# Depthwise convolution moved from ScalarE and GpSimd to TensorE, one tap at a time between other matmuls

## The chip, the core and the metric

The kernel runs on one core of a Trainium2 chip. The metric is the device time of one execution in microseconds (us); the number given is the median of several. The engines of the core are named as in the profile: PE is TensorE (PEld its weight loads), DVE is VectorE, ACT is ScalarE, POOL is GpSimd, and SP is the engine whose queue issues the DMAs. PE writes its results to PSUM, which has eight banks of 512 float32 per partition; everything else lies in SBUF.

## The reference

Two layers of an encoder trunk work on 512 prompt positions and on 8 streams of 16 positions each, 640 columns in all. Each layer is a half-step feed-forward block, a token mixer and a second half-step feed-forward block. The mixer has three groups: sparse attention with an indexer that selects the top 128 or 132 keys of each query, a gated linear recurrence, and a convolution module. The change touches the last:

```python
def conformer_conv(glu, buf, conv_w, conv_b, ln_g, ln_b):
    a, gate = jnp.split(glu, 2, axis=-1)
    u = a * jax.nn.sigmoid(gate)
    u_pad = jnp.concatenate([buf.astype(u.dtype), u], axis=1)
    y = lax.conv_general_dilated(u_pad, conv_w[:, None, :], window_strides=(1,), padding='VALID',
                                 feature_group_count=C_CONV) + conv_b      # 31 taps, 256 channels
    y = jax.nn.silu(layer_norm(y, ln_g, ln_b))
```

Beside it the indexer's scores are `sum over heads of w * relu(qi . ki)`, of which the largest are selected; the recurrence is a sum over pairs of positions within a chunk, each with the product of the decays between them.

## The kernel before

Channels lie on the partitions and the 640 positions along the free axis, so the 256 channels of the convolution are two groups `g` of 128 partitions. All arithmetic is float32. Each layer runs as a row of blocks with a barrier between them; the block in question is `select_and_recur` (line 728), once per layer. Each engine has its own instruction list in it and waits on semaphores.

PE (line 870) first transposes some tiles (line 873), then computes 24 logit products, `for n, (t, hd) in enumerate(units)` (line 884): one matmul of 256, 384 or 512 columns each (line 892), in a ring of three banks. ACT takes each through a relu (line 1033), and DVE adds it, weighted, to the scores (lines 1099 and 1102). Then come the eight streams (line 899): logits of stream b (lines 908 and 909, four half-size matmuls), a relu on ACT (line 1051), and a weighting matmul of 512 and one of 16 columns, one iteration later (lines 917 and 919); the last of them completes the count `mixed`.

The recurrence is computed by levels m = 0, 1, 2, 4, 8, 16, 32. `prods` lists 33 level products, five in each of the levels up to 8 and four in each of the last two; each is two matmuls of 256 columns (line 938) into bank `n % 8`. DVE waits until a level's products are all there (line 1173), then folds the decays into the operands `qz` and `kp` for the next level (line 1178 for m = 0, lines 1199, 1203 and 1205 otherwise), which PE needs before it starts that level's products, then copies the level's products out of PSUM (lines 1160 and 1164), and then does one or two selection steps.

A selection step finds and removes the eight largest scores in each live row block: `max` (line 1129) and `match_replace` (line 1139). There are 28 steps for the streams and the prompt together: 12 ahead of the levels, of which the last takes the streams' scores (line 1124, after `mixed`), the rest beside the levels and behind them. DVE then makes the masks (line 1223) and the states of the recurrence (lines 1231 to 1255), PE the outputs of the recurrence (lines 980 to 1002).

The convolution runs beside this. POOL first makes the gated input `up` and `us` (lines 842 and 844). ACT scales it by one tap, for the prompt and the streams (`scale_tap`, lines 1017 and 1018), into a ring of three buffers `product`, and POOL adds the product to `yc` (line 860): 62 scalings and 60 additions per layer. ACT issues two scalings beside each stream's relu and the rest behind.

Of the kernel before, what the change touches and what calls it, by code (L numbers as in the profile page):

```python
# [63 lines left out]
def build(nc, ins, outs):  # L64
    stack = ExitStack()
    with stack:
# [661 lines left out]
        def select_and_recur(l):  # L728
# [2 lines left out]
            rb = carve(3, LALL)  # L731
            wall = carve(NS, 128)
            icb = carve(2, PAST)
            product = carve(3, TOK)
            top8 = carve(4, 8)
            s0 = carve(NS, 2, 128)
            kiz = arena[:, ARENA - 1024:ARENA - 1024 + SEQ]
            qis = proj[:, NPROJ, 0:512].rearrange("p (b n) -> p b n", b=NS)
            (tok_mm, vnew_mm, wall_mm, tok_ready, vnew_ready, wall_ready, kid_ready, logits, relu_done, weighed,
             mixed, barred, topped, replaced, masks, ic_in, gate_sig, glu_ready, conv_in, padded, conv_out, tap_scaled,  # L740
             tap_added) = (
                sem(f"sel_{n}") for n in (
                    "tok_mm", "vnew_mm", "wall_mm", "tok_ready", "vnew_ready", "wall_ready", "kid_ready", "logits",
                    "relu_done", "weighed", "mixed", "barred", "topped", "replaced", "masks", "ic_in", "gate_sig",
                    "glu_ready", "conv_in", "padded", "conv_out", "tap_scaled", "tap_added"))
            ic_in1, qis_ready, tabs_in = sem("sel_ic_in1"), sem("sel_qis_ready"), sem("sel_tabs_in")
            ic_sems = [ic_in, ic_in1]
            units = [(t, hd) for t in range(1, NEW) for hd in range(8)]
# [24 lines left out]
            o = mix[:, 4:6]  # L773
            um = flat(proj[:, 0:4])[:, 0:2048].rearrange("p (b g n) -> p b g n", b=NS, g=2)
            snew = im.rearrange("p g b n -> p (g b n)").rearrange("p (b g n) -> p b g n", b=NS, g=2)
            osq = product[:, 0:2]
            (s0_in, q_act, sig_f, sig_k, gate_act, lb_ready, f_ready, k_ready, level_mm, scored, folded_q, folded_k,
             folded_t, im_ready, kst_mm, kst_ready, u_mm, u_ready, state, new_ready, o_mm, o_copied,
             o_squared, osum_mm, oroot, saved) = (sem(f"rec_{n}") for n in (
# [17 lines left out]
            with nc.Block() as block:  # L797
# [35 lines left out]
                @block.gpsimd  # L833
                def _(pool):
                    pool.memset(kid[0:64], 0.0).then_inc(padded, 1)
                    pool.wait_ge(padded, 1)
                    pool.memset(kiz[64:128], 0.0).then_inc(padded, 1)
                    pool.wait_ge(padded, 2)
                    pool.memset(up[:, :, 0:TAPS - 1], 0.0).then_inc(padded, 1)
                    for g in range(2):  # L840
                        pool.wait_ge(gate_sig, g + 1)
                        pool.tensor_tensor(up[:, g, TAPS - 1:], proj[:, CA + g, 0:SEQ], proj[:, CG + g, 0:SEQ],
                                           ALU.mult).then_inc(glu_ready, 1)
                        pool.tensor_tensor(us[:, g, :, TAPS - 1:],
                                           proj[:, CA + g, SEQ:].rearrange("p (b i) -> p b i", b=NS),
                                           proj[:, CG + g, SEQ:].rearrange("p (b i) -> p b i", b=NS),
                                           ALU.mult).then_inc(glu_ready, 1)
                    pool.wait_ge(logits, NIDX)
                    pool.wait_ge(qis_ready, 1)
                    for rows_, a in own:  # L850
                        pool.memset(qz[rows_, :, 1 - a], 0.0).then_inc(padded, 1)
                        pool.wait_ge(padded, 4 + a)

                    for g in range(2):
                        for w in range(1, TAPS):
                            n = g * (TAPS - 1) + w - 1
                            pool.wait_ge(tap_scaled, g * TAPS + w + 1)
                            if w >= 2:
                                pool.wait_ge(tap_added, n)
                            pool.tensor_tensor(yc[:, g], yc[:, g], product[:, n % 3], ALU.add).then_inc(tap_added, 1)  # L860
                    pool.wait_ge(mixed, NS)

                    for g in range(2):
                        pool.tensor_tensor(im[:, g],
                                           tok[:, 4:5, 128 + 128 * g:256 + 128 * g].to_broadcast([128, NS, 128]),
                                           batchmask.unsqueeze(2).to_broadcast([128, NS, 128]),
                                           ALU.mult).then_inc(im_ready, 1)

                @block.tensor
                def _(pe):  # L870
# [4 lines left out]
                    for b in range(NS):  # L875
# [1 line left out]
                                          proj[:, VA, SEQ + LS * b:SEQ + LS * b + LS], ident)  # L877
                    mm.then_inc(vnew_mm, 1)
                    pe.matmul(ps[:, 7, 0:128], headsel[64:72, :], proj[64:72, KI, SEQ:], start=True,
                              stop=True).then_inc(wall_mm, 1)  # L880

                    pe.wait_ge(kid_ready, 2)
                    pe.wait_ge(padded, 3)
                    for n, (t, hd) in enumerate(units):
                        keys, _ = keys_of(t)
                        if n < 3:
                            pe.wait_ge(tok_ready, n + 1)
                        else:
                            pe.wait_ge(relu_done, n - 2)

                        ki = kid if hd % 2 else kiz
                        pe.matmul(ps[:, n % 3, 0:keys], proj[:, QI + hd // 2, 128 * t:128 * t + 128], ki[:, 0:keys],
                                  start=True, stop=True).then_inc(logits, 1)

                    pe.wait_ge(tok_ready, 5)
                    pe.wait_ge(vnew_ready, 2)
# [2 lines left out]
                    for b in range(NS + 1):  # L899
# [13 lines left out]
                        if b > 0:  # L913
# [4 lines left out]
                                      stop=(c == NS - 1))  # L918
                            pe.matmul(ps[:, 5, 0:LS], wall[:, c], rb[:, (NIDX + c) % 3, PAST:], start=(c == 0),
                                      stop=(c == NS - 1)).then_inc(mixed, 1)  # L920

                    for n, (m, t) in enumerate(prods):
                        if n == 4:
# [7 lines left out]
                        else:  # L931
                            i = levels.index(m) - 1
                            pe.wait_ge(folded_q, fold_count(i))
                            pe.wait_ge(folded_k, fold_count(i) - 1)
                        if n >= 8:
                            pe.wait_ge(scored, n - 7)
                        for g in range(2):
                            mm = pe.matmul(ps[:, n % 8, 256 * g:256 * g + 256], kp[:, g, 128 * t:128 * t + 128],  # L938
                                           qz[:, g, :, 128 * t:128 * t + 128], start=True, stop=True)
                        mm.then_inc(level_mm, 1)  # L940

                    pe.wait_ge(scored, NP)
                    pe.wait_ge(folded_k, fold_count(6) - 1)
# [61 lines left out]

                @block.scalar
                def _(act):
                    def scale_tap(m):

                        g, w = divmod(m, TAPS)  # L1010
                        n = g * (TAPS - 1) + w - 1
                        tap, *srcs = tap_of(g, w)
                        if w and n >= 3:
                            act.wait_ge(tap_added, n - 2)
                        outs_ = conv_parts(product[:, n % 3] if w else yc[:, g])
                        bias = par[:, P_CB + g:P_CB + g + 1] if w == 0 else 0.0
                        act.activation(outs_[0], srcs[0], ACT.Identity, scale=tap, bias=bias)  # L1017
                        act.activation(outs_[1], srcs[1], ACT.Identity, scale=tap, bias=bias).then_inc(tap_scaled, 1)  # L1018
# [9 lines left out]
                    for n, (t, hd) in enumerate(units):  # L1028
                        keys, _ = keys_of(t)
                        act.wait_ge(logits, n + 1)  # L1030
                        if n >= 3:
                            act.wait_ge(weighed, n - 2)
                        act.activation(rb[:, n % 3, 0:keys], ps[:, n % 3, 0:keys], ACT.Relu).then_inc(relu_done, 1)

                    act.wait_ge(tok_mm, 5)
                    act.activation(flat(f), flat(kp), ACT.Sigmoid).then_inc(sig_f, 1)
# [6 lines left out]
                    for b in range(NS):  # L1043
# [8 lines left out]
                        if b == 0:  # L1052
                            act.wait_ge(glu_ready, 4)
                            act.wait_ge(padded, 3)
                            act.wait_ge(conv_in, 32)
                        scale_tap(2 * b)
                        scale_tap(2 * b + 1)
                    for m in range(2 * NS, 2 * TAPS):
                        scale_tap(m)
                    for t in range(5):  # L1060
                        act.wait_ge(kst_mm, t + 1)
                        act.activation(kst[:, t], ps[:, t, 0:256].rearrange("p (g n) -> p g n", g=2),
                                       ACT.Copy).then_inc(kst_ready, 1)
                    act.wait_ge(tap_added, 2 * (TAPS - 1))
                    for n, t in enumerate((4, 0, 1, 2, 3)):
                        act.wait_ge(o_mm, n + 1)
                        src = ps[:, n % 4, 0:256].rearrange("p (g n) -> p g n", g=2)
# [7 lines left out]
                def _(dve):  # L1075
# [8 lines left out]
                    dve.wait_ge(wall_mm, 1)  # L1084
# [69 lines left out]
                    def keep_scores(i, m, at, k):  # L1154

                        t = prods[at + k][1]
                        dst = sc[:, t].rearrange("p (a g i) -> p g a i", a=2, g=2)
                        src = ps[:, (at + k) % 8].rearrange("p (g a i) -> p g a i", g=2, a=2)
# [559 lines left out]
```

## Time and profile before

| | before |
|---|---|
| median of 3 runs | 3256.18 us (3256.08 to 3257.55) |
| span of the profiled execution, first to last instruction | 3254.3 us |
| PE busy | 2851.5 us, 88% of the span |
| DVE busy | 1528.1 us, 47% |
| ACT busy | 944.0 us, 29% |
| POOL busy | 476.2 us, 15% |
| the block of layer 1 | 744.0 to 944 us of the span |
| the block of layer 2 | 2332 to 2532 us of the span |

The profile gives no time of the profiled execution other than its span; what lies around the span is taken as the difference to the median, 1.9 us. Busy shares are averages over the whole execution: nearly all of PE's time lies in the feed-forward blocks, which the change does not touch. The 200 us blocks have to be read by themselves.

### The profile page before, as it was taken

The numbers are of one execution on the slowest core, as the hardware profiler recorded it, in microseconds if no ns is written. First come the engines' busy times: TensorE is split into PE (matmuls) and PEld (weight loads), VectorE is DVE, ScalarE is ACT, GpSimd is POOL, SyncE is SP. The second block draws the span as 40 slices with busy tenths as digits, with TensorE's granted clock in tenths as the row PEclk, the third lists the DMA queues.
The fourth block names the chain that finished last, engine by engine and source line by source line (L and its number), as shares of the span: only waits on it lengthen the run. The fifth ranks groups of instructions, "written<-read, shape, count | busy, mean of one in ns | idle before, by whom it ended". The sixth has DMA issues, their size and how long they took to land. (4 is left out here: it accounts for less than half of the span.)

```text
span 3254.3 us, 44093 instructions
## 1 busy us (share of the span) xinstructions
PE 2851.5 (88%) x18054; PEld 2665.5 (82%) x18054; DVE 1528.1 (47%) x1886; ACT 944.0 (29%) x1237; POOL 476.2 (15%) x328
## 2 busy tenths in 40 slices
PE   1999998997477979999969999989955788999997
PEld 1899998894354879999969999979834458999997
DVE  1633333528965353333353333352499644433333
ACT  1322223216423332212232212231362342322221
POOL 1100001105812120000120000020084313000001
PEclk9999999998768989999989999999976798999998
DMA  5122212113010212122112122122120111212211
GB/s 108 65 71 71 78 63 79 65 52 98 1 73 7 72 52 78 59 83 73 57 60 84 62 81 77 57 73 78 36 76 15 59 46 46 78 68 75 78 61 63
DMA packets 50676, 209.51 MB, mean 64 GB/s; under 512 B 13928, under 2 KB 14312, under 8 KB 34568
## 3 DMA queue, kind: packets, MB, share of 16 engines
q1 hardware_dynamic: 50568, 208.05, 19.3%
q8 instruction: 70, 1.15, 0.1%
q14 instruction: 38, 0.31, 0.0%
HBM read 197.85 MB, written 10.19 MB: 64 GB/s over the span
## 5 line engine op out<-in xcount | busy, mean ns | idle before, releaser
L291 PE MATMUL ps<-hr,wr 128*128 128x320 f32 x11424 | 1707.5, 311 | 83.6 <-DVE hr L407 65.7
L291 PEld LDWEIGHTS ps<-hr,wr 128*128 128x128 f32 x11424 | 1692.3, 189 | 99.7 <-DVE hr L407 43.5
L291 PE MATMUL ps<-hid,wr 128*128 128x320 f32 x4224 | 620.8, 309 | 0.0
L291 PEld LDWEIGHTS ps<-hid,wr 128*128 128x128 f32 x4224 | 619.8, 188 | 0.0
L286 DVE TENSOR_TENSOR wr<-stage,wr 128x2048 fp32r<-128x2048 f32 x184 | 421.7, 2292 | 299.7 <-ACT wr L282 299.7
L282 ACT ACTIVATE wr<-stage 128x2048 fp32r<-128x2048 f32 x184 | 350.6, 1905 | 557.5 <-PE ps L291 288.9
L548 DVE TENSOR_TENSOR arena<-ps,arena 128x640 f32<-128x640 f32 x88 | 72.5, 824 | 545.5 <-PE ps L291 543.8
L523 POOL TENSOR_TENSOR arena<-arena 128x640 f32<-128x640 f32 x28 | 44.3, 1582 | 1737.0 <-ACT arena L499 1737.0
L490 ACT ACTIVATE arena<-arena 128x640 f32<-128x640 f32 x88 | 65.1, 739 | 801.8 <-DVE arena L548 801.8
L860 POOL TENSOR_TENSOR proj<-proj,arena 128x640 f32<-128x640 f32 x120 | 200.1, 1669 | 33.6 <-ACT arena L1018 16.9
L938 PE MATMUL ps<-proj 128*128 128x256 f32 x264 | 90.9, 519 | 97.5 <-issue 78.4
L938 PEld LDWEIGHTS ps<-proj 128*128 128x128 f32 x264 | 70.2, 273 | 117.5 <-issue 82.1
L556 DVE TENSOR_TENSOR hid<-arena,hid 128x640 f32 x88 | 72.6, 825 | 91.8 <-ACT hid L492 91.8
L1017 ACT ACTIVATE arena<-arena,par 128x512 f32<-128x512 f32 x120 | 86.5, 721 | 79.6 <-POOL proj L860 79.6
L380 POOL TENSOR_TENSOR arena<-arena 128x640 f32<-128x640 f32 x48 | 95.6, 1992 | 85.9 <-ACT arena L367 82.4
L563 DVE COPY arena<-ps 128x640 f32 x32 | 26.4, 825 | 164.0 <-PE ps L291 164.0
L621 DVE TENSOR_TENSOR proj<-ps,arena 128x640 f32 x20 | 16.5, 825 | 171.6 <-PE ps L291 171.0
L1428 ACT ACTIVATE arena<-arena 128x128 f32<-128x128 f32 (+4 forms) x80 | 47.7, 596 | 154.4 <-DVE arena L1486 154.4
L492 ACT ACTIVATE hid<-arena 128x640 f32 x88 | 65.1, 740 | 92.7 <-DVE arena L554 92.7
L336 PE MATMUL ps<-ones,arena 128*128 128x1 f32 x70 | 17.6, 320 | 84.7 <-DMA par<-in_params 66.4
L336 PEld LDWEIGHTS ps<-ones,arena 128*128 128x128 f32 x70 | 16.2, 286 | 87.3 <-DMA par<-in_params 67.9
L499 ACT ACTIVATE arena<-arena 128x640 f32 (+1 forms) x32 | 23.6, 739 | 196.3 <-DVE arena L565 196.3
(204 smaller groups left out, 2224.5 us busy)
## 6 DMA issues: line engine op xcount, KB each, us to landing
stage<-in_wgu SPq DMA_DIRECT2D x88, 1024.0 KB, 4.8
stage<-in_wd SPq DMA_DIRECT2D x32, 768.0 KB, 4.2
stage<-in_w_in SPq DMA_DIRECT2D x24, 1024.0 KB, 4.8
stage<-in_wd SPq DMA_DIRECT2D x32, 640.0 KB, 3.8
stage<-in_w_out SPq DMA_DIRECT2D x8, 1024.0 KB, 5.0
arena<-in_ic SPq DMA_DIRECT2D x16, 256.0 KB, 2.8
hf<-bias_table SPq DMA_DIRECT2D x2, 2048.0 KB, 10.7
arena<-in_kc SPq DMA_DIRECT2D x16, 256.0 KB, 5.2
```

What stands on the lines that cost most here:

```text
L282: act.activation(wr[:, j, 0], stage[:, j], ACT.Copy).then_inc(w_hi, 1)
L286: dve.tensor_tensor(wr[:, j, 1], stage[:, j], wr[:, j, 0].bitcast(F32), ALU.subtract).then_inc(w_lo, 1)
L291: mm = pe.matmul(out, w(s), v(t), start=start and n == 0, stop=stop and n == 2)
L380: pool.tensor_tensor(ssum, ssum, sqb[:, k % 2], ALU.add).then_inc(self.summed, 1)
L490: act.activation(sg[:, 0], sg[:, 0], ACT.Silu).then_inc(silu, 1)
L492: act.activation(hid_view(i, j, 0), sg[:, 1], ACT.Copy).then_inc(hid_hi, 1)
L548: dve.tensor_tensor(halves(sg[:, 0]), ps[:, 4 * j:4 * j + 2, 0:HALF], rs2, ALU.mult).then_inc(g_scaled, 1)
L556: dve.tensor_tensor(hid_view(i, j, 1), sg[:, 1], hid_view(i, j, 0).bitcast(F32), ALU.subtract).then_inc(hid_ready, 1)
L860: pool.tensor_tensor(yc[:, g], yc[:, g], product[:, n % 3], ALU.add).then_inc(tap_added, 1)
L938: mm = pe.matmul(ps[:, n % 8, 256 * g:256 * g + 256], kp[:, g, 128 * t:128 * t + 128], qz[:, g, :, 128 * t:128 * t + 128], start=True, sto ...
L1017: act.activation(outs_[0], srcs[0], ACT.Identity, scale=tap, bias=bias)
L1428: act.activation(pb[:, u % 3, 0:keys], pb[:, u % 3, 0:keys], ACT.Exp, scale=-1.0, bias=low[:, u:u + 1], accum_out=norm[:, u:u + 1]).then_i ...
```

## The change

For each group and tap ACT makes a 128x128 matrix with the tap's 128 weights on the diagonal (`diagonal`, in a ring of five buffers). PE multiplies the gated input, shifted by the tap, with it, once for the prompt (512 columns, bank 6) and once for the streams (128 columns, bank 7), and accumulates the 31 taps of a group in PSUM (`conv_tap`). One such tap is put behind each logit product from the fifth on (taps 0 to 19), behind each of the nine iterations over the streams (20 to 28) and behind each level product (29 to 61). ACT copies a finished group out of PSUM with the bias added (`conv_to_sbuf`); the first tap of the second group waits for that. The level products use a ring of six banks in place of eight. The scalings on ACT and the additions on POOL are gone.

```diff
@@ gpsimd
-                    for g in range(2):
-                        for w in range(1, TAPS):
...
-                            pool.tensor_tensor(yc[:, g], yc[:, g], product[:, n % 3], ALU.add).then_inc(tap_added, 1)
@@ tensor
+                    def conv_tap(m):
+                        g, w = divmod(m, TAPS)
+                        _, prompt, sample = tap_of(g, w)
+                        if m == 0:
+                            pe.wait_ge(vnew_ready, 2)
+                            pe.wait_ge(wall_ready, 1)
+                            pe.wait_ge(glu_ready, 4)
+                            pe.wait_ge(padded, 3)
+                            pe.wait_ge(conv_in, 32)
+                        if w == 0 and g:
+                            pe.wait_ge(conv_done, g)
+                        pe.wait_ge(diag_ready, m + 1)
+                        pe.matmul(ps[:, 6, :], diag[:, m % NDIAG], prompt, start=(w == 0), stop=(w == TAPS - 1))
+                        pe.matmul(ps[:, 7, 0:NS * LS], diag[:, m % NDIAG], sample, start=(w == 0),
+                                  stop=(w == TAPS - 1)).then_inc(tap_mm, 1)
@@ the logit products
+                        if n >= 4:
+                            conv_tap(n - 4)
@@ the streams
+                        conv_tap(NIDX + b - 4)
@@ the level products
-                        if n >= 8:
-                            pe.wait_ge(scored, n - 7)
+                        if n >= NBANK:
+                            pe.wait_ge(scored, n - NBANK + 1)
...
                         mm.then_inc(level_mm, 1)
+                        conv_tap(NIDX + NS + 1 + n - 4)
@@ scalar
-                    def scale_tap(m):
...
+                    def diagonal(m):
+                        g, w = divmod(m, TAPS)
+                        tap, *_ = tap_of(g, w)
+                        if m >= NDIAG:
+                            act.wait_ge(tap_mm, m - NDIAG + 1)
+                        act.activation(diag[:, m % NDIAG], ident, ACT.Identity, scale=tap).then_inc(diag_ready, 1)
+                    def conv_to_sbuf(g):
+                        act.wait_ge(tap_mm, TAPS * (g + 1))
+                        act.wait_ge(glu_ready, 4)
+                        bias = par[:, P_CB + g:P_CB + g + 1]
+                        act.activation(yc[:, g, 0:SEQ], ps[:, 6, :], ACT.Identity, bias=bias)
+                        act.activation(yc[:, g, SEQ:], ps[:, 7, 0:NS * LS], ACT.Identity, bias=bias).then_inc(conv_done, 1)
...
                         act.activation(rb[:, n % 3, 0:keys], ps[:, n % 3, 0:keys], ACT.Relu).then_inc(relu_done, 1)
+                        if n >= 1:
+                            diagonal(n - 1)
...
-                        scale_tap(2 * b)
-                        scale_tap(2 * b + 1)
-                    for m in range(2 * NS, 2 * TAPS):
-                        scale_tap(m)
+                        diagonal(n - 1)
+                    for m in range(NIDX + NS - 1, 2 * TAPS):
+                        diagonal(m)
+                        if m == TAPS + 1:
+                            conv_to_sbuf(0)
+                    conv_to_sbuf(1)
...
-                    act.wait_ge(tap_added, 2 * (TAPS - 1))
```

## Rows read from the trace of the kernel before

**Rows 1.** Windows of layer 1's block: length, busy us of each engine, PEclk, DMA.

```profile
core 0: us, PE busy (x) PEld busy (x) DVE busy (x) ACT busy (x) POOL busy (x), PEclk, DMA share, GB/s
744.00:766.00 22.00, 20.01 (x80) 11.91 (x82) 19.14 (x38) 16.23 (x31) 5.48 (x8) 1.00 0.23 60
766.00:796.50 30.50, 21.73 (x96) 10.82 (x97) 29.86 (x92) 26.40 (x45) 20.25 (x15) 0.83 0.48 157
796.50:898.50 102.00, 45.70 (x133) 35.25 (x133) 100.83 (x158) 47.63 (x94) 85.36 (x50) 0.72 0.09 19
898.50:944.00 45.50, 35.00 (x162) 25.75 (x162) 28.58 (x55) 7.53 (x17) 0.00 (x0) 0.62 0.07 26
```

**Rows 2.** Timeline of DVE, levels of layer 1: start, us, line, operation [idle before].

```profile
802.81 0.69 DVE L1124 COPY arena<-ps 128x528 f32<-128x528 f32 x1
...
807.80 4.27 DVE L1178 TENSOR_TENSOR proj<-proj 64x1280 f32<-64x1280 f32 x2
...
819.35 3.62 DVE L1199 TENSOR_TENSOR proj<-proj 64x640 f32<-64x640 f32 x2
...
834.38 3.49 DVE L1199 TENSOR_TENSOR proj<-proj,arena 64x640 f32<-64x640 f32 x2
...
841.61 3.21 DVE L1164 COPY_PREDICATED hf<-lvl,ps 128x512 f32<-128x512 int32 x5
...
848.94 3.67 DVE L1199 TENSOR_TENSOR proj<-proj,arena 64x640 f32<-64x640 f32 x2
...
875.96 2.10 DVE L1199 TENSOR_TENSOR proj<-proj,stage 64x256 f32<-64x256 f32 x2 [0.60 <-PE ps L938]
...
891.97 0.84 DVE L1199 TENSOR_TENSOR proj<-proj,stage 64x256 f32<-64x256 f32 x2
892.84 0.42 DVE L1203 TENSOR_TENSOR proj<-proj,stage 128x256 f32<-128x256 f32 x1
...
894.55 1.49 DVE L1209 TENSOR_TENSOR proj<-proj 128x1280 f32<-128x1280 f32 x1
...
913.46 2.48 DVE L1231 TENSOR_TENSOR proj<-ps,cst 128x512 f32<-128x512 f32 x4
```

**Rows 3.** Timeline of POOL in layer 1's block.

```profile
750.93 0.51 POOL L844 TENSOR_TENSOR arena<-proj 128x128 f32<-128x128 f32 x1
...
776.05 108.52 POOL L860 TENSOR_TENSOR proj<-proj,arena 128x640 f32<-128x640 f32 x60 [8.47 <-ACT arena L1018]
```

**Rows 4.** Timeline of PE and ACT, logit products of layer 1.

```profile
751.67 13.47 PE L892 MATMUL ps<-arena,proj 128*128 128x256 f32 x36 [1.17 <-ACT arena L1033]
...
764.32 0.60 ACT L1033 ACTIVATE arena<-ps 128x512 f32<-128x512 f32 x1 [0.26 <-PE ps L892]
765.17 0.60 ACT L1033 ACTIVATE arena<-ps 128x512 f32<-128x512 f32 x1 [0.26 <-PE ps L892]
```

**Rows 5.** Timeline of PE, sums of one column each at the full clock.

```profile
558.17 0.35 PE L336 MATMUL ps<-ones,arena 128*128 128x1 f32 x2 [1.94 <-PEq L437]
558.38 0.36 PE L337 MATMUL ps<-ones,arena 128*128 128x1 f32 x2
```

**Rows 6.** The page's costliest groups: form, count, busy us, mean ns, idle before.

```profile
L1018 ACT ACTIVATE arena<-arena,par 128x128 f32<-128x128 f32 x120 | 46.9, 391 | 0.0
```

**Rows 7.** Timeline of ACT and PE, streams of layer 1.

```profile
773.30 0.59 ACT L1051 ACTIVATE arena<-ps 128x528 f32<-128x528 f32 x1
...
773.95 2.07 PE L917 MATMUL ps<-arena 128*128 128x512 f32 x2 [5.90 <-ACT arena L1051]
...
781.12 1.12 PE L917 MATMUL ps<-arena 128*128 128x512 f32 x2
...
783.39 1.12 PE L917 MATMUL ps<-arena 128*128 128x512 f32 x2
```

**Rows 8.** Timeline of PE, level products of layer 1.

```profile
803.56 1.13 PE L938 MATMUL ps<-proj 128*128 128x256 f32 x4 [1.62 <-DVE arena L1124]
...
840.05 6.68 PE L938 MATMUL ps<-proj 128*128 128x256 f32 x20 [7.60 <-issue]
```

**Rows 9.** A window within the logit products of layer 1, columns as in Rows 1.

```profile
750.00:753.00 3.00, 1.83 (x8) 0.85 (x7) 2.58 (x5) 1.15 (x4) 1.45 (x2) 1.00 0.03 11
```

More of the change, by code:

```diff
@@ L733, in select_and_recur @@
             icb = carve(2, PAST)
-            product = carve(3, TOK)
+            osq = carve(2, TOK)
+            NDIAG, NBANK = 5, 6
+            diag = carve(NDIAG, 128)
             top8 = carve(4, 8)
@@ L738, in select_and_recur @@
             qis = proj[:, NPROJ, 0:512].rearrange("p (b n) -> p b n", b=NS)
-            (tok_mm, vnew_mm, wall_mm, tok_ready, vnew_ready, wall_ready, kid_ready, logits, relu_done, weighed,
-             mixed, barred, topped, replaced, masks, ic_in, gate_sig, glu_ready, conv_in, padded, conv_out, tap_scaled,
-             tap_added) = (
+            (tok_mm, vnew_mm, tok_ready, vnew_ready, wall_ready, kid_ready, logits, relu_done, weighed,
+             mixed, barred, topped, replaced, masks, ic_in, gate_sig, glu_ready, conv_in, padded, conv_out, diag_ready,
+             tap_mm, conv_done) = (
                 sem(f"sel_{n}") for n in (
-                    "tok_mm", "vnew_mm", "wall_mm", "tok_ready", "vnew_ready", "wall_ready", "kid_ready", "logits",
+                    "tok_mm", "vnew_mm", "tok_ready", "vnew_ready", "wall_ready", "kid_ready", "logits",
                     "relu_done", "weighed", "mixed", "barred", "topped", "replaced", "masks", "ic_in", "gate_sig",
-                    "glu_ready", "conv_in", "padded", "conv_out", "tap_scaled", "tap_added"))
+                    "glu_ready", "conv_in", "padded", "conv_out", "diag_ready", "tap_mm", "conv_done"))
             ic_in1, qis_ready, tabs_in = sem("sel_ic_in1"), sem("sel_qis_ready"), sem("sel_tabs_in")
@@ L775, in select_and_recur @@
             snew = im.rearrange("p g b n -> p (g b n)").rearrange("p (b g n) -> p b g n", b=NS, g=2)
-            osq = product[:, 0:2]
             (s0_in, q_act, sig_f, sig_k, gate_act, lb_ready, f_ready, k_ready, level_mm, scored, folded_q, folded_k,
@@ L852, in _ @@
                         pool.wait_ge(padded, 4 + a)
-                    for g in range(2):
-                        for w in range(1, TAPS):
[L856 to L859, printed above, removed]
-                            pool.tensor_tensor(yc[:, g], yc[:, g], product[:, n % 3], ALU.add).then_inc(tap_added, 1)
                     pool.wait_ge(mixed, NS)
@@ L879, in _ @@
                     pe.matmul(ps[:, 7, 0:128], headsel[64:72, :], proj[64:72, KI, SEQ:], start=True,
-                              stop=True).then_inc(wall_mm, 1)
+                              stop=True).then_inc(vnew_mm, 1)
+                    def conv_tap(m):
[13 more added lines that the diff above has]
+                                  stop=(w == TAPS - 1)).then_inc(tap_mm, 1)
                     pe.wait_ge(kid_ready, 2)
@@ L934, in _ @@
                             pe.wait_ge(folded_k, fold_count(i) - 1)
-                        if n >= 8:
-                            pe.wait_ge(scored, n - 7)
+                        if n >= NBANK:
+                            pe.wait_ge(scored, n - NBANK + 1)
                         for g in range(2):
-                            mm = pe.matmul(ps[:, n % 8, 256 * g:256 * g + 256], kp[:, g, 128 * t:128 * t + 128],
+                            mm = pe.matmul(ps[:, n % NBANK, 256 * g:256 * g + 256], kp[:, g, 128 * t:128 * t + 128],
                                            qz[:, g, :, 128 * t:128 * t + 128], start=True, stop=True)
                         mm.then_inc(level_mm, 1)
+                        conv_tap(NIDX + NS + 1 + n - 4)
                     pe.wait_ge(scored, NP)
@@ L1007, in _ @@
                 def _(act):
-                    def scale_tap(m):
+                    def diagonal(m):
                         g, w = divmod(m, TAPS)
[L1011 to L1018, printed above, removed]
+                        tap, *_ = tap_of(g, w)
[8 more added lines that the diff above has]
+                        act.activation(yc[:, g, SEQ:], ps[:, 7, 0:NS * LS], ACT.Identity, bias=bias).then_inc(conv_done, 1)
                     act.activation(kid[64:128, :], proj[0:64, KI], ACT.Copy).then_inc(kid_ready, 1)
@@ L1051, in _ @@
                         act.activation(rb[:, n % 3], flat(ps[:, q:q + 2])[:, 0:LALL], ACT.Relu).then_inc(relu_done, 1)
[L1052 to L1055, printed above, removed]
-                        scale_tap(2 * b)
-                        scale_tap(2 * b + 1)
-                    for m in range(2 * NS, 2 * TAPS):
-                        scale_tap(m)
+                        diagonal(n - 1)
[4 more added lines that the diff above has]
+                    conv_to_sbuf(1)
                     for t in range(5):
@@ L1083, in _ @@
                                         ps[0:LS, 5 + a, :].rearrange("p (b n) -> p b n", b=4)).then_inc(vnew_ready, 1)
-                    dve.wait_ge(wall_mm, 1)
+                    dve.wait_ge(vnew_mm, 2)
                     dve.wait_ge(tabs_in, 16)
@@ L1157, in keep_scores @@
                         dst = sc[:, t].rearrange("p (a g i) -> p g a i", a=2, g=2)
-                        src = ps[:, (at + k) % 8].rearrange("p (g a i) -> p g a i", g=2, a=2)
+                        src = ps[:, (at + k) % NBANK].rearrange("p (g a i) -> p g a i", g=2, a=2)
                         if m == 0:
```

## The prediction

> **What bounds the kernel now.** I read the page's busy shares first and then left them: 88% of PE's time lies mostly in the feed-forward blocks, which the change leaves alone. Both blocks that it touches take 200 us, and layer 2 repeats layer 1 within 0.1 us at every mark I compared, so I work on layer 1 and double. The windows by stage [rows 1] show which engine ends last in each: in the logit products PE is busy 20.0 of 22 us; from there to the end of the levels DVE is busy 29.9 of 30.5 and 100.8 of 102 us; in the tail PE again. So a change is worth something if it shortens DVE's list between 766 and 898 us, or PE's before and after it. ACT and POOL end nowhere last: taking work from them buys nothing by itself.
>
> Next I read DVE's timeline in the levels for operations whose price varies. The pair at line 1199 on 64x256 takes 2.10 us at 875.96 and 0.84 us at 891.97, the same shape [rows 2]. What differs is POOL: its additions run from 776.05 for 108.5 us, to 884.6 [rows 3]. The same holds for line 1203. Copies out of PSUM and selection steps don't show it. So POOL's additions, which nobody waits for, lengthen DVE's folds, whose two inputs both lie in SBUF. That is where the change can gain.
>
> **The price of a tap on PE.** A 512-column float32 matmul costs 0.86 us at the full clock: the relus of two successive logit products, which wait for PE, are 0.85 to 0.86 us apart [rows 4]. The 128-column part is two passes like any float32 matmul; by columns that is a quarter, 0.21 us, and the pairs that only load weights and stream one column are 0.21 to 0.22 us apart [rows 5], so 0.22 either way. A tap is 1.08 us. Bounds: 0.86 if the 128 columns hide entirely; 1.29 if a load shows at two of the four passes (0.11 each, half of that pair). I take 1.08, since in the logit products loads are hidden.
>
> The Trainium skill ("TensorE: Matmul & The Clock Gate", Part 3, "The mechanism") says that weight loads overlap matmuls in flight only when they address other rows of the array. Diagonals fill all rows. By that rule every load would show, and a tap would cost far more; here the rule does not agree with rows 4, where full-height logit products follow each other at their column time. It stands as a rival below.
>
> **Logit stage: added, on the path.** The first tap waits for POOL's gated input, which ends at 751.4 [rows 3]; PE is then at its sixth product, where it now stands at 751.67 [rows 4]. Before the last logit 19 taps stand: 19 x 1.08 = 20.5 us, and 0.3 for the order. PE is already the bound, so nothing hides this; DVE has nothing else to do, since selection needs all scores. ACT adds a diagonal (0.39 us, some 0.3 from start to start [rows 6]) beside each relu; that fits in a 1.5 to 1.9 us unit, but the last one stands ahead of the sigmoids on which DVE's next step waits: 0.3. Selection starts **21.1 us late**.
>
> **Streams: nearly hidden.** ACT's first stream relu moves from 773.30 to 794.4, the weighting from 773.95 to 795.05. Its first two rounds take 7.17 us, partly at half clock (773.95 to 781.12), then 2.27 each [rows 7]. With taps: 7.17 + 3.2 (one tap at half clock, one at full), then 5 x (2.27 + 1.08) = 16.8, then 1.2 for the last weighting: 823.4. DVE takes the scores at 802.81 [rows 2] + 21.1 = 823.9. So the taps just fit, with 0.5 us to spare. Behind that stand tap 28 and four level products each with a tap, 1.08 + 4 x 1.94 = 8.8, 0.3 for the first tap of the second group, which waits for ACT's two copies out of PSUM (0.60 [rows 4] and 0.3 [rows 6], and the way there and back, against a level product of 0.86), and a lone fifth product at 1.13 [rows 8]: 833.7. DVE would be ready at 807.80 + 21.1 = 828.9, and now waits 4.8 us, which it did not. The first fold is **25.9 us late**.
>
> **Levels: the gain.** Without POOL a 64- or 128-row fold costs 0.42 us at 256 elements and 1.49 at 1280 [rows 2], so 0.82 at 640. From a fold's start to PE's release: 2 x 1.45 = 2.9 us at m = 0; 3 x 0.82 = 2.46 at m = 1 to 8; 2.58 at m = 16, as at 891.97 to 894.55. Today PE's products hide behind copies and selection, 848.94 - 841.61 = 7.3 us. With taps they don't: five products with four taps take 5 x 0.86 + 4 x 1.08 + 0.27 (fill and drain, from the lone product, 1.13 - 0.86) = 8.9; four with three take 7.0. The fifth tap runs beside the next fold. So each level is now PE's: fold plus products, 0.1 for the two semaphores.
>
> m = 0: 2.9 + 8.9 + 0.1 = 11.9 against 11.55 (807.80 to 819.35), +0.35. m = 1, 2, 4, 8: 3 x 11.45 + 9.5 = 43.85 against 56.61 (819.35 to 875.96), -12.8. m = 16: 9.6 against 16.0 (875.96 to 891.97), -6.4. From 891.97 to 913.46 POOL was already still: 0. Sum **-18.85**. DVE's folds alone would have given some 27; PE's bursts take the rest back.
>
> Edits at nothing: six banks (the next product waits for a copy that follows the fold at once, 0.7 us per copy against 1.94 per product and tap); the removed wait for POOL at ACT's line 1064 (POOL's last addition ends well ahead of the tail [rows 3]); SP's loads behind the streams' logits, the level masks among them, move by 21 to 25 us like their users; POOL's later operations come earlier. The copy of the second group has the rest of DVE's selection as cover.
>
> **Sum.** 25.9 - 18.85 = +7.05 us per layer, +14.1 for two. The profiled span of 3254.3 becomes 3268.4; with the 1.9 us that the median lies above the span, **3270 us**. Terms of this size err by 2 to 4 us per layer.
>
> **Rivals.**
> *The sample half is free* (faster): a tap costs 0.86. Some 19 + 4 + 22 taps lie on the path, plus 4 in the streams: 49 x 0.22 x 2 = -21.6, 3249 us. For it: both halves use the same diagonal. Against: two such matmuls on one weight (lines 917 and 919) load it anew each, and rows 5. It decides below 0.87 us per tap. Chance 0.12.
> *The clock falls between bursts*: PE now rests 1.4 to 1.8 us at each fold. After 7.6 us of rest a burst took 6.68 us in place of 4.57 at the full clock [rows 8]; six such losses of 2.1 us per layer are +25, 3295 us. Against: a rest of 1.17 us left the clock at 1.00 [rows 4, 9]. Chance 0.11. The Trainium skill (same page, "A second HAM failure mode: psum-queue depth-cycling") tells of a kernel whose short rests between groups kept its clock swinging; no row here has this rhythm.
> *Loads show*: a tap at 1.29, 0.21 x 49 x 2 = +20.6, 3291 us. Chance 0.11.
> *Every load shows*: with 0.11 us at each of a tap's four passes a tap is 0.86 + 0.21 + 0.44 = 1.51, 0.43 x 49 x 2 = +42, 3312 us. Against: rows 4. Chance 0.02. This is the rule of the skill named above.
> *The folds stay slow* (the change doesn't do what it says): a fold releases PE after 5.5 us, 5.5 + 9.0 is the old interval, so only the delay stays: +27.7 per layer, 3311 us. The equal shapes in rows 2 speak against. Chance 0.04.
>
> **How the numbers follow.** The forecast case has 0.60. Its terms leave it between 3258 and 3280; 0.2% (6.5 us), about what a measurement of this kernel can tell from no change, puts 0.18 of it at "same" and 0.42 at "slower". Slower: 0.42 + 0.11 + 0.11 + 0.02 + 0.04 = 0.70; faster 0.12. The range leaves out the first rival and the last two, 0.18: 3254 to 3296.
>
> **What would show it.** The after profile should have no POOL in the levels; folds at 0.42 and 0.82 us each; 19 taps pushing the last logit's relu from 765.17 to 786; taps 1.08 us apart; DVE idle in the levels with PE named as releaser, 1 to 2 us per level and some 5 us before the first fold; the granted clock at 1.00 in the levels. A clock near 0.7 there, or a tap off 1.08, would make the time wrong; a logit stage that didn't grow would make the reasoning wrong.

## The result

| | before | after |
|---|---|---|
| median | 3257.55 us (3254.05 to 3263.14) | 3268.6 us (3266.4 to 3270.19) |
| ratio to before, 95% interval | | 1.0034 (1.0023 to 1.0045) |
| span of the profiled execution | 3254.3 us | 3267.2 us |
| DVE busy | 1528.1 us | 1475.5 us |
| ACT busy | 944.0 us | 865.4 us |
| POOL busy | 476.2 us | 275.8 us |

The changed kernel is slower by 11 us, though ACT, POOL and DVE together have some 330 us less to do; PE has 109 us more. The two blocks account for most of it. From its first matmul to the end of its last sums on PE the block runs 4.97 us longer than before in layer 1 and 5.97 us in layer 2: 10.94 us of the 12.9 us between the two spans. The other 2.0 us come from stretches that the change does not touch: 1.31 us more ahead of layer 1's block, whose first matmul starts at 745.35 in place of 744.04, 1.8 us less between the two blocks, and 2.5 us more behind the second. To compare marks of layer 1 with those of before, take 1.31 off.

The windows of layer 1's block after the change, columns as in [rows 1], cut at the end of the logit products, at DVE's copy of the streams' scores and behind the last fold:

```profile
745.30:788.20 42.90, 41.27 (x160) 24.31 (x160) 19.86 (x39) 22.68 (x54) 5.65 (x8) 1.00 0.12 31
788.20:825.10 36.90, 32.34 (x138) 16.84 (x138) 36.01 (x109) 15.06 (x24) 3.47 (x4) 0.91 0.44 146
825.10:904.80 79.70, 64.98 (x260) 44.45 (x258) 66.55 (x138) 13.22 (x33) 1.62 (x1) 0.99 0.09 16
```

The first stage has doubled and PE fills it (41.27 of 42.90 us). In the third DVE waits: it is busy 66.6 of 79.7 us, where it was busy 93.6 of 94.8 us between the same marks before (802.8 to 897.6). POOL's share of it has shrunk from 79.5 us to 1.6.

PE in the logit stage (timeline: start, us, line, operation). L903 is a logit product, L889 and L890 are the two halves of a tap:

```profile
784.20 1.02 PE L903 MATMUL ps<-arena,proj 128*128 128x512 f32 x2
785.05 1.02 PE L889 MATMUL ps<-arena 128*128 128x512 f32 x2
785.91 0.38 PE L890 MATMUL ps<-arena 128*128 128x128 f32 x2
786.13 1.02 PE L903 MATMUL ps<-arena,proj 128*128 128x512 f32 x2
```

From start to start the tap takes 0.86 + 0.22 = 1.08 us, and product and tap 1.93 us together. DVE from the copy of the streams' scores to the states (L1195 and L1216 are the folds):

```profile
825.11 0.70 DVE L1141 COPY arena<-ps 128x528 f32<-128x528 f32 x1
...
833.19 2.99 DVE L1195 TENSOR_TENSOR proj<-proj 64x1280 f32<-64x1280 f32 x2 [3.00 <-issue]
...
845.20 1.66 DVE L1216 TENSOR_TENSOR proj<-proj 64x640 f32<-64x640 f32 x2 [1.67 <-PE ps L952]
...
856.76 1.66 DVE L1216 TENSOR_TENSOR proj<-proj,arena 64x640 f32<-64x640 f32 x2 [1.00 <-PE ps L952]
...
868.31 1.65 DVE L1216 TENSOR_TENSOR proj<-proj,arena 64x640 f32<-64x640 f32 x2 [1.33 <-PE ps L952]
...
879.87 1.66 DVE L1216 TENSOR_TENSOR proj<-proj,stage 64x640 f32<-64x640 f32 x2 [1.51 <-PE ps L952]
...
889.48 0.85 DVE L1216 TENSOR_TENSOR proj<-proj,stage 64x256 f32<-64x256 f32 x2 [2.48 <-PE ps L952]
...
899.19 0.85 DVE L1216 TENSOR_TENSOR proj<-proj,stage 64x256 f32<-64x256 f32 x2 [1.59 <-PE ps L952]
...
920.70 2.48 DVE L1248 TENSOR_TENSOR proj<-ps,cst 128x512 f32<-128x512 f32 x4
```

The folds behind the first cost less than half of what they did in [rows 2]: 1.66 us for 3.49 to 3.67, 0.85 for 2.10 (the first 2.99 for 4.27). But each of them now stands behind a wait for PE's level products (L952), 1.0 to 2.5 us. The row at 833.19 names no releaser for its 3.00 us; PE's side shows it:

```profile
796.26 2.08 PE L930 MATMUL ps<-arena 128*128 128x512 f32 x2 [4.56 <-ACT arena L1071]
...
798.41 2.06 PE L889 MATMUL ps<-arena 128*128 128x512 f32 x2
...
800.83 1.30 PE L921 MATMUL ps<-arena,proj 64*64 64x512 f32 x4
...
802.13 1.13 PE L930 MATMUL ps<-arena 128*128 128x512 f32 x2
...
805.58 1.13 PE L930 MATMUL ps<-arena 128*128 128x512 f32 x2
...
819.38 1.13 PE L930 MATMUL ps<-arena 128*128 128x512 f32 x2
...
821.67 1.02 PE L930 MATMUL ps<-arena 128*128 128x512 f32 x2
...
822.66 1.10 PE L889 MATMUL ps<-arena 128*128 128x512 f32 x2
...
832.07 1.03 PE L952 MATMUL ps<-proj 128*128 128x256 f32 x4
...
836.23 1.13 PE L952 MATMUL ps<-proj 128*128 128x256 f32 x4 [2.06 <-DVE proj L1195]
...
847.81 1.10 PE L952 MATMUL ps<-proj 128*128 128x256 f32 x4 [1.56 <-DVE proj L1216]
```

The fifth product of level 0 starts at 832.07 and lasts 1.03 us; the fold starts at 833.19, right behind it. Then PE waits for the fold, and DVE for the five products with their taps: a closed loop of 11.56 us for a level of five products.

### The profile page after: what moved, and what is told of

It reads as the page before. It is cut to its first block and busy times, and to the rows that moved or that the text cites. A ratio compares the mean times of both kernels' runs of the same rounds, so it can differ in the third digit from the quotient of the medians.

```text
span 3267.2 us, 44745 instructions
## 1 busy us (share of the span) xinstructions
PE 2960.4 (91%) x18550; PEld 2726.8 (83%) x18550; DVE 1475.5 (45%) x1886; ACT 865.4 (26%) x1121; POOL 275.8 (8%) x208
## 3 DMA queue, kind: packets, MB, share of 16 engines
q8 instruction: 74, 1.21, 0.2%
## 5 line engine op out<-in xcount | busy, mean ns | idle before, releaser
L889 PE MATMUL ps<-arena 128*128 128x512 f32 x248 | 130.5, 608 | 3.5 <-POOL arena L845 3.2
L563 DVE COPY arena<-ps 128x640 f32 x32 | 26.4, 825 | 164.0 <-PE ps L291 164.0
L890 PEld LDWEIGHTS ps<-arena 128*128 128x128 f32 x248 | 47.5, 192 | 60.6 <-issue 60.6
L952 PE MATMUL ps<-proj 128*128 128x256 f32 x264 | 68.7, 383 | 20.0 <-DVE proj L1216 15.9
L554 DVE TENSOR_TENSOR arena<-arena 128x640 f32<-128x640 f32 x88 | 72.7, 826 | 12.7 <-ACT arena L490 0.2
```

Of the source, the lines that this page charges most:

```text
L554: dve.tensor_tensor(sg[:, 1], sg[:, 0], sg[:, 1], ALU.mult).then_inc(hid_done, 1)
L889: pe.matmul(ps[:, 6, :], diag[:, m % NDIAG], prompt, start=(w == 0), stop=(w == TAPS - 1))
L952: mm = pe.matmul(ps[:, n % NBANK, 256 * g:256 * g + 256], kp[:, g, 128 * t:128 * t + 128], qz[:, g, :, 128 * t:128 * t + 128], start=True, ...
```

## The experiments

The theory was the forecast's own: taps at 1.08 us on PE's path ahead of the selection and inside each level, against folds that are cheap once POOL no longer adds beside them. The first five kernels below take these apart, the sixth is the ring by itself, and the seventh puts together what the first three suggest. The kernel before had a median of 3257.03 us beside experiments 1, 2, 3 and 7 and of 3256.54 us beside 4, 5 and 6, at most 1.0 us under its 3257.55 beside the changed kernel.

**1. The taps ahead of the selection.** Edit to the changed kernel:

```diff
-                        if n >= 4:
-                            conv_tap(n - 4)
```

and the counts of the remaining 42 taps moved to match.

> The changed kernel with the 20 taps behind the logit products left out (taps 0 to 19 of the first channel group are not computed), the other 42 as they were. Theory: these taps stand on the path, since PE bounds the logit products and DVE has nothing else to do; the last logit's relu comes back by 19 x 1.08 + 0.3 = 21 us per layer, everything behind it keeps its distance, and the time falls from 3268.6 to about 3227 us (0.991 of before). Rival: the logit stage was waiting for something else (POOL's gated input, ACT's diagonals) and the taps filled that wait; then the time falls by less than 10 us.

Measured: 3225.96 us (3223.61 to 3227.34), 0.9899 of before (0.9883 to 0.9916), 42.6 us under the changed kernel: 21.3 per layer. DVE's selection and first fold:

```profile
769.78 1.48 DVE L1145 MAX8 arena<-arena 128x8 f32<-128x256 f32 x3
...
809.68 2.99 DVE L1194 TENSOR_TENSOR proj<-proj 64x1280 f32<-64x1280 f32 x2 [2.26 <-issue]
```

Its block starts 2.05 us earlier than in the changed kernel, where the selection begins at 792.55. So the selection is 792.55 - 769.78 - 2.05 = 20.7 us earlier, and the first fold 833.19 - 809.68 - 2.05 = 21.5. All of the stage's growth is path. Without these taps the change would have been faster than before.

**2. POOL's additions, almost taken away.** Edit to the kernel before, so that POOL adds 16 of 640 columns and the rest of the sums is left out:

```diff
-                            pool.tensor_tensor(yc[:, g], yc[:, g], product[:, n % 3], ALU.add).then_inc(tap_added, 1)
+                            pool.tensor_tensor(yc[:, g, 0:16], yc[:, g, 0:16], product[:, n % 3, 0:16],
+                                               ALU.add).then_inc(tap_added, 1)
```

> The kernel before with each of POOL's 60 additions per layer cut from 640 to 16 columns (the rest of the convolution's sum is left out); all waits, all scalings on ACT and all of PE's work stay. Theory: the folds are slow only because POOL's additions run beside them; line 1199 on 64x640 falls from 1.8 to 0.83 us each, the stretch from the first fold to the last level's shrinks by some 25 to 27 us per layer, and the time is 3203 to 3208 us (0.985). Rival: the folds are slow because of ACT's scalings, or of the strided operands: then the folds and the time stay (3257 us).

Measured: 3203.91 us (3200.94 to 3208.27), 0.9833 of before (0.9814 to 0.9852). ACT still issues all 62 scalings, PE has no tap, and the order is unchanged. DVE in the levels, and one of POOL's additions beside it:

```profile
807.86 2.99 DVE L1179 TENSOR_TENSOR proj<-proj 64x1280 f32<-64x1280 f32 x2
...
818.11 1.66 DVE L1200 TENSOR_TENSOR proj<-proj 64x640 f32<-64x640 f32 x2
...
863.91 0.85 DVE L1200 TENSOR_TENSOR proj<-proj,stage 64x256 f32<-64x256 f32 x2
```

```profile
817.53 0.22 POOL L860 TENSOR_TENSOR proj<-proj,arena 128x16 f32<-128x16 f32 x1 [0.69 <-ACT arena L1019]
818.43 0.58 POOL L860 TENSOR_TENSOR proj<-proj,arena 128x16 f32<-128x16 f32 x1 [0.68 <-ACT arena L1019]
```

The folds are at the changed kernel's price, from the first fold to that of the last level (m = 32) it is 56.05 us in place of 84.17 [rows 2], and even the tiny addition that falls into a fold at 818.43 takes 0.58 us and not 0.22. The long folds come from POOL's additions: with ACT's scalings and the strided operands as they were, nothing of them is left. In layer 2 the same stretch takes 57.84 us, since one fold waits 1.81 us for PE. This kernel shows nearly the whole prize, 53 us for both layers. The changed kernel collects 18 us per layer in the levels and pays 24 ahead of them.

The Trainium skill ("SBUF — State Buffer", "Who interferes with whom") says that a DVE instruction with two SBUF inputs contends with a GpSimd instruction that reads SBUF, and that the order of issue decides which of the two blocks. The trace agrees on both sides: 2.10 against 0.84 us for DVE's fold, 0.58 against 0.22 us for POOL's addition.

**3. The level taps in another place.** Edit to the changed kernel: the same taps, but all behind the level's last product instead of one behind each.

```diff
-                        conv_tap(NIDX + NS + 1 + n - 4)
+                        if n == first[m] + count[m] - 1:
+                            for j in range(first[m], n + 1):
+                                conv_tap(NIDX + NS + 1 + j - 4)
```

> The changed kernel with one edit: the taps of a level stand behind the level's last product, not between its products; all 62 taps are computed. Theory: in the levels PE's burst is the bound only because four taps stand ahead of the product that DVE waits for; behind it they run beside DVE's copies, selection and next fold. A level is then 10 to 10.7 us for m = 1 to 4 (was 11.56), 7.4 for m = 8 (9.6), and the first fold starts 2 to 3 us earlier: -12 us per layer, 3245 us, below before (0.996). Rival: the taps only move, and delay the next level's first product by as much as they no longer delay the last: 3268 us.

Measured: 3241.91 us (3238.84 to 3243.01), 0.9947 of before (0.9930 to 0.9964): 26.7 us under the changed kernel. DVE and PE:

```profile
827.51 2.98 DVE L1197 TENSOR_TENSOR proj<-proj 64x1280 f32<-64x1280 f32 x2
...
837.76 1.65 DVE L1218 TENSOR_TENSOR proj<-proj 64x640 f32<-64x640 f32 x2
...
883.37 0.84 DVE L1218 TENSOR_TENSOR proj<-proj,stage 64x256 f32<-64x256 f32 x2
```

```profile
832.25 4.48 PE L952 MATMUL ps<-proj 128*128 128x256 f32 x20
836.57 1.02 PE L889 MATMUL ps<-arena 128*128 128x512 f32 x2
```

No fold waits for PE. The first fold to the last level's takes 55.86 us in place of 66.00, as in experiment 2, and the stall before the first fold is gone (3.1 us): 13.2 us per layer, 26.4 for two. PE does the same number of taps; they now run while DVE copies and selects, 5 taps (5.4 us) in cover that was always there. The price of a level tap was its place, not its work.

**4. The level taps left out.** Edit to the changed kernel: the 33 taps behind the level products are not done, so the second group's convolution and two taps of the first are missing; ACT's matrices for them and its copy of the second group are gone too.

> The changed kernel with the 33 taps from the level products on left out, so most of the second group's convolution is not computed. Theory (in the levels PE's burst of products and taps stands on the path, the folds are at their uncontended price): the intervals from fold to fold return to those of the kernel whose POOL additions were cut to 16 columns, 56.0 us from the first fold to the sixth level's in place of 66.0, and the 3.0 us stall before the first fold goes: -13 per layer, 3243 us, with the tail perhaps 1 us per layer longer because PE is colder. Rival (the clock of PE decides: with long rests it falls to about 0.7, and the products take 1.5 times as long, 6.7 us a burst): half of the gain is lost, some 3255 us. Second rival (the interval is set by something other than the taps): 3268 us.

Measured: 3244.7 us (3242.06 to 3249.28), 0.9969 of before (0.9959 to 0.9979): 23.9 us under the changed kernel. It is no faster than experiment 3, which does those taps. Layer 1's levels (825 to 905) have a mean granted clock of 0.79, against 0.99 with the taps in the changed kernel, and one interval shows it:

```profile
873.88 6.74 PE L952 MATMUL ps<-proj 128*128 128x256 f32 x16 [5.35 <-DVE proj L1211]
883.37 5.38 PE L952 MATMUL ps<-proj 128*128 128x256 f32 x16 [2.75 <-DVE proj L1211]
```

```profile
880.66 0.85 DVE L1211 TENSOR_TENSOR proj<-proj,stage 64x256 f32<-64x256 f32 x2 [2.27 <-PE ps L952]
```

Sixteen level matmuls take 6.74 us after a rest of 5.35 us, and there DVE waits 2.27 us for them. The first fold to the last level's (the expectation counts it as the sixth) is 58.5 us in layer 1 and 56.8 in layer 2, against 56.0 expected. So the theory holds. The rival of the falling clock is worth 1 to 2.5 us per layer when PE rests long, not the half of the gain, some 6 us per layer, that the expectation gave it.

**5. The price of the 128-column half.** Edit to the changed kernel:

```diff
-                        pe.matmul(ps[:, 7, 0:NS * LS], diag[:, m % NDIAG], sample, start=(w == 0),
-                                  stop=(w == TAPS - 1)).then_inc(tap_mm, 1)
```

with the signal moved to the prompt's half.

> The changed kernel with the 128-column matmul of every tap left out, so the convolution of the sample tokens is not computed. Forecast's theory (a tap costs 0.86 + 0.22 us): 19 taps before the selection give back 19 x 0.22 = 4.2 us per layer, the stall before the first fold (3.0 us) shrinks by about 2.9, some 23 level taps give back 5.1: -12.2 per layer, 3244 us. Rival (the 128-column half hides under the 512-column one, and a tap costs its 1.08 us for another reason): no change, 3268 us. A result under 3238 would say that the second half costs more than its own 0.22, by a reload or a drain.

Measured: 3247.38 us (3244.92 to 3249.06), 0.9974 of before (0.9965 to 0.9984): 21.2 us under the changed kernel, 3.4 us less than expected. DVE's marks, its block starting 2.60 us earlier than the changed kernel's:

```profile
785.61 1.47 DVE L1145 MAX8 arena<-arena 128x8 f32<-128x256 f32 x3
...
823.70 2.99 DVE L1194 TENSOR_TENSOR proj<-proj 64x1280 f32<-64x1280 f32 x2 [0.45 <-issue]
...
884.65 0.85 DVE L1215 TENSOR_TENSOR proj<-proj,stage 64x256 f32<-64x256 f32 x2 [0.91 <-PE ps L951]
```

The selection starts 792.55 - 785.61 - 2.60 = 4.34 us earlier, which is 0.228 us for each of 19 taps. The stall falls from 3.00 to 0.45, and first fold to last takes 60.95 us in place of 66.00. Together 11.9 us in layer 1 (expected 12.2); behind the levels 0.5 us go back, since the block's last sums on PE take 4.22 us and not 3.67. Layer 2 gives back less: the block is 10.8 us shorter (11.4 in layer 1), and there the fold of m = 1 waits 2.45 us for PE, whose granted clock is 0.87 around that level (2405 to 2418; 1.00 in layer 1). The half is neither free nor dearer than its columns. Without it the change would stand where the rival of the free sample half put it.

**6. The ring of six banks alone.** Edit to the kernel before: `n % 8` becomes `n % 6`, and a product waits for the sixth before it.

> The kernel before with its level products in six PSUM banks in place of eight, nothing else. Forecast's theory: a product waits for the copy or selection six products back, which is done long before, so there is no change: 3257 us, within 4. Rival (the ring is what holds products back in a level): the sixth product of a row waits, a few us per level, over 3265 us.

Measured: 3261.31 us (3254.15 to 3262.98), 1.0010 of before (0.9999 to 1.0020). The interval just holds no change, and the median is 4.8 us up, a little more than the 4 that the expectation allowed. In the trace the block of layer 1 starts 1.21 us later than in the kernel before, ahead of any edit, and its marks keep that distance or less:

```profile
808.99 4.27 DVE L1178 TENSOR_TENSOR proj<-proj 64x1280 f32<-64x1280 f32 x2
...
892.91 0.84 DVE L1199 TENSOR_TENSOR proj<-proj,stage 64x256 f32<-64x256 f32 x2
...
914.41 2.48 DVE L1231 TENSOR_TENSOR proj<-ps,cst 128x512 f32<-128x512 f32 x4
```

1.19, 0.94 and 0.95 us behind [rows 2]. In layer 2 the distance grows inside the block, from 1.83 us at its start to 3.84 at the last level's fold. The fold of m = 16 waits 1.15 us where it waited 0.23, for sixteen level matmuls that take 7.00 us in place of 6.10, at a granted clock of 0.63 between 2453 and 2467 in place of 0.71:

```profile
2466.27 2.97 DVE L1199 TENSOR_TENSOR proj<-proj,stage 64x256 f32<-64x256 f32 x2 [1.15 <-PE ps L938]
```

None of those sixteen waits for a bank. In the levels of m = 2, 4 and 8 the second product does wait for a copy, in both layers and for 0.23 to 0.73 us, which the expectation did not have; no fold comes later by it, and in layer 1 of the changed kernel no product waits so. So the rival's few us per level are ruled out, and layer 1 shows no cost; a cost of a few us in all is not ruled out, as the interval reaches 1.0020. The run also shows that some 1.2 us ahead of the block, as seen in the changed kernel, come without the change.

**7. Both lessons together.** If POOL's additions hurt only beside the folds, and taps only ahead of the selection and inside a level, each can have the stretch in which it hurts nobody. ACT and POOL do the first 17 taps of the first group while DVE selects, as before the change. PE does the other 45: five beside the first two streams' logits, ahead of the first weighting, one behind each weighting, and the rest behind the last product of each level. One more accumulating pass with the identity adds POOL's sum to PE's. POOL's two later products (L868), which follow its additions, wait for the end of the levels here, so POOL is still in all of them. The edit's main lines:

```diff
+            conv_seq = [(0, w) for w in range(NPOOL, TAPS)] + [None] + [(1, w) for w in range(TAPS)]
+            BEHIND = {0: 2, 1: 5, 2: 5, 4: 5, 8: 5, 16: 4, 32: 7}
...
-                        if n >= 4:
-                            conv_tap(n - 4)
...
-                        conv_tap(NIDX + NS + 1 + n - 4)
+                        if n == first[m] + count[m] - 1:
+                            conv_taps(BEHIND[m])
```

> All 62 taps are computed, in other places: no tap beside the logit products; ACT and POOL do the first 17 taps of group 0 while DVE only selects (POOL must be still when the first fold starts); PE does the other 45 plus one pass with the identity that adds POOL's partial sum, 5 ahead of the first weighting of the streams, 8 beside the streams, 33 behind the levels' last products. Theory (logit taps cost 21 us per layer, POOL slows only folds, taps behind a level are hidden): the first fold starts where it did before (807.8 in layer 1), the folds are short, no level waits for PE by more than 1 us; 27 us per layer less than before, 3203 to 3208 us (0.985). If POOL is late or the streams are too long, the first fold comes some us later and each costs double in the total.

Measured: 3201.6 us (3199.13 to 3206.1), 0.9823 of before (0.9806 to 0.9839), faster than both kernels and level with experiment 2, which leaves the sums out. POOL's additions, and two windows (selection with the streams; levels):

```profile
776.51 26.89 POOL L864 TENSOR_TENSOR proj<-proj,arena 128x640 f32<-128x640 f32 x16 [8.76 <-ACT arena L1055]
```

```profile
766.00:803.00 37.00, 36.80 (x164) 20.26 (x164) 36.37 (x111) 31.44 (x60) 26.03 (x18) 1.00 0.50 171
803.00:868.00 65.00, 60.29 (x238) 41.97 (x239) 64.42 (x136) 11.78 (x30) 0.40 (x1) 0.97 0.08 6
```

POOL ends at 803.4, before the first fold at 807.96. In the levels PE is busy 60.3 of 65 us and DVE 64.4: PE is nearly full, and no fold waits for it. Against experiment 2 the convolution costs nothing that can be measured. That kernel is no exact floor, since it still scales on ACT and adds 16 columns on POOL, and its layer 2 waits once for PE; a kernel without any convolution was not run.

## Why the prediction came out right

The forecast was 3270 us with the direction "slower", and the time is 3268.6. Its terms, per layer:

| term | forecast | layer 1 | layer 2 |
|---|---|---|---|
| selection starts later | +21.1 | +21.00 | +21.02 |
| first fold later still (the stall) | +4.8 | +3.08 | +2.85 |
| levels up to m = 16 | -18.85 | -18.17 | -17.91 |
| from there to the states | 0 | +0.02 | 0 |
| tail of the block | 0 | -0.96 | +0.01 |
| sum | +7.05 | +4.97 | +5.97 |

The mechanism is the one that was forecast, and so is the size of its terms but for the second and, in layer 1, the tail. Layer 2's levels gain 0.3 us less, since its last fold came 0.25 us earlier than layer 1's already before the change. That the total agrees within 1.4 us is in part luck: the two blocks grew by 10.9 us and not by 14.1, 2.0 us came from stretches that the change does not touch, and the kernel before, measured again, took 1.4 us more than the 3256.18 that the forecast started from.

**The tap.** 1.08 us, so that the 19 taps give 20.5 us; experiments 1 and 5 confirm it from two sides (20.7 us for 19 taps, 0.228 for the 128 columns). The rival of the loads that show would have needed 1.29. The Trainium skill ("TensorE: Matmul & The Clock Gate", Part 3, "The mechanism") has the rule as the prediction took it, that a load overlaps matmuls in flight only where the row groups differ, and one paragraph above names a second way, a load into the background weight buffer. The trace does not agree with the "only": PE has as many weight loads as matmuls in the logit stage (160 of each), those of taps and logit products are full-height, and a 512-column half still takes its 0.86 us. The second way would allow that; no run here shows the buffer itself.

**The stall, the one term that was mis-sized.** I let the streams end 0.5 us ahead of DVE's need. They ended 2.4 us ahead (the tap behind the last weighting starts at 822.66, DVE's copy at 825.11): from the first weighting to there I had 28.4 us, and PE took 26.4. Half of that lies in the first two rounds, where I added a tap at half clock and one at full to [rows 7], 10.4 us; they took 9.3 (796.26 to 805.58). PE has no gap in them, with the taps or without, and in both kernels the granted clock is 0.50 at the first weighting. It is back at 1.00 some 5.6 us later before the change and 5.1 us later with the taps. So the taps did not lengthen the stretch at half clock, and two of them added 2.15 us, their price at the full clock. The other half is in the later rounds: I gave all five the price of a round with a stream's logits, but the last has none and takes 2.29 us (819.38 to 821.67); the four before it were dearer than forecast, 3.45 us for 3.35. What is left, the stall itself, has the cause that was named: experiment 3 removes it by moving the taps.

**The levels.** 12.01 us at m = 0, 11.56 for the next three, 9.61 and 9.71, each 0.1 above the forecast. Together they shrink by 18.2 us and not 18.85. Bursts with taps, not the clock, set them: PE rests 1.56 us at a fold (2.06 at m = 0) and the granted clock is 0.99, close to its upper level of 2.4 GHz. The swing that the Trainium skill tells of (same page, "A second HAM failure mode: psum-queue depth-cycling") does not appear at this rhythm.

**The tail.** Not forecast. The block's last sums on PE ran faster in layer 1, and not in layer 2, at a granted clock of 0.66 against 0.50:

```profile
945.54 3.67 PE L1017 MATMUL ps<-arena,cst 128*128 128x320 f32 x8 [0.48 <-ACT arena L1085]
...
2536.40 4.64 PE L1017 MATMUL ps<-arena,cst 128*128 128x320 f32 x8 [0.48 <-ACT arena L1085]
```

Before the change both took 4.64 us. The wait ahead of both is the same 0.48 us; why the clock came back earlier in one layer was not tried and stays open.

**What the forecast did not ask.** It priced the placement that was given and found it a loss. The gain of 27 us per layer that it named for DVE's folds was real (28 in layer 1 of experiment 2), and nothing forced PE to give it back: the cover stood in its own text, 7.3 us of copies and selection per level, in which the products hid before. Products and taps together (4.3 + 5.4 us) fit a level of some 10 us, if the products come first, as experiment 3 shows.

## What to carry to other kernels

Work that is moved to an idle engine is not free there: ask for each piece which wait of that engine ends last at the place where it is put, and put it behind the result that another engine is waiting for, not ahead of it. Look for engines off the critical path that lengthen the operations on it: the same shape at two prices in one timeline is the sign, and the cheapest test is to shrink the suspect's operation without changing the order. When two engines each hurt in only one stretch, split the work by stretch before choosing one of them.

## What the runs showed that was not expected

A kernel that does 33 taps more per layer in its levels was no slower than the one without them (3241.9 against 3244.7 us): between 825.1 and 886 us the granted clock was 1.00 with them and 0.81 without, and one burst of sixteen level matmuls took 6.74 us. With taps around it the same burst takes 3.61, as here in the kernel of experiment 7:

```profile
851.81 3.61 PE L975 MATMUL ps<-proj 128*128 128x256 f32 x16
```

A tap ahead of the half-size matmuls of a stream shows about 0.1 us more than one ahead of a full-size matmul: its 128-column half starts at 787.86 and the next matmul at 788.18, 0.32 us against 0.22 in the logit stage. That is the tenth by which the rounds were under-priced.

```profile
787.86 0.39 PE L890 MATMUL ps<-arena 128*128 128x128 f32 x2
788.18 1.08 PE L921 MATMUL ps<-arena,proj 64*64 64x512 f32 x4
```
